# Four-layer decoder trunk on one core: the chunks of the feed-forward loop taken in pairs in layers 2 to 4

## The chip, the cores and the metric

The kernel runs on one core of one Trainium2 chip. The metric is the time of one execution on the device in microseconds. A core has TensorE (PE, with its weight loads shown apart as PEld), VectorE (DVE), ScalarE (ACT), GpSimd (POOL) and SyncE (SP), which here only issues transfers of weights. They work on their own queues, each in order, and wait for one another by semaphores.

## The reference

Four layers over x of 256 tokens by 1024 channels, in float32. Each layer has a token mixer (forgetting attention in the first and fourth, a state-space layer in the second, causal mean pooling in the third), and then a gated feed-forward part:

```python
def swiglu(x, w1, w3, w2):
    return (jax.nn.silu(x @ w1) * (x @ w3)) @ w2
...
    for i in range(DEPTH):
        ...   # m = the mixer of layer i, applied to h
        h = layer_norm(DN_ALPHA * h + m, ln_g[i, 0], ln_b[i, 0])
        h = layer_norm(DN_ALPHA * h + swiglu(h, ffn_w1[i], ffn_w3[i], ffn_w2[i]), ln_g[i, 1], ln_b[i, 1])
```

w1 and w3 are 1024 x 2816, w2 is 2816 x 1024.

## The kernel before

**Weights as tiles.** All weights are cut into 370 tiles of 128 x 1024 float32 (512 KB), numbered in the order in which they are used. Each tile goes through four steps. SyncE brings it from memory into one of four places of `raw`; it issues the transfer of tile c once the low half of tile c-4 is made. ScalarE makes the tile's high half (line 616, `whi` or `ext`, type float32r), VectorE the low half, raw minus high (line 1020). TensorE then multiplies with the halves, three products for each full one: high by high, high by low, low by high.

**Places and the ring.** A pair of halves lies in one of eight places (four in `whi`/`wlo`, four in `ext`) in this part of the program. The function `ring` deals them out in turn, and the high half of tile c waits until the tile that had the place before it has been used (`before[c]`), as a rule tile c-8. At three tiles, `SKIPS = (starts[2] - 40, starts[2] + 12, starts[3] + 12)`, the order of the places is turned by two, so the six tiles from there on take the place of the tile six back, and the two behind them that of the tile fourteen back. The first of these, starts[2]-40, is tile 26 of the second layer's feed-forward part. The other two are in the mixers of the third and fourth layer.

**The feed-forward part.** The 2816 hidden channels are 22 chunks (`FCH`) of 128. A chunk c has three tiles: up 1 (w1) makes 128 x 256 in PSUM bank 4, up 3 (w3) the same in bank 5, with 24 matmuls of 256 columns each (lines 1627 to 1629), and down (w2) adds h @ w2 into banks 0 to 3, with 14 matmuls (lines 1636 to 1661). T0 is the number of the layer's first such tile, T_FFN = 66 their count. The first two chunks are done together by other code; chunks 2 to 21 go through `up1`, `up3` and `down` on TensorE:

- up1(c) waits for silu of chunk c-1 (`silu_ready`), which has read bank 4.
- ScalarE: silu of bank 4 (line 697), after up1(c). VectorE: product of bank 5 and silu into `hval` (line 1168), after up3(c). up3(c+1) waits for it (`h_ready`).
- h is split as the weights are: ScalarE copies `hval` to h's high half (line 702), VectorE makes the low half (line 1172). down(c) waits for it (`hlo_ready`). The halves lie in `hhi`/`hlo`, two places by c % 2; the last two chunks of a layer have `h3hi`, `h3lo`, `h4hi`, `h4lo`.

The place of a tile in the order is given by `up_at(c)` (up 1; up 3 is one behind it) and `down_at(c)`. On TensorE, down(c-1) comes behind up 3 of chunk c, for c from 3 to 18. Chunks 19, 20 and 21 have their six up tiles in a row, and the remaining down tiles come last, in `tm_end`.

**What stands between on ScalarE and VectorE.** In `chunk(c)` each splits weights on the way, up to a tile given by u = T0 + up_at(c): up to u+7 ahead of silu (or of the product), up to u+8 ahead of h's half, up to u+9 behind it (the 7 is 3 + L, with L = AHEAD = 4 in layers 2 to 4). A half in that queue that has to wait for its transfer or its place holds up what is behind it:

```python
split_to(u + 3 + L)
act.wait_ge(w_used, u + 1)
nc.scalar.activation(silu[:, :], bank[4][:, 0:SEQ], ACT.Silu).then_inc(silu_ready, 1)
split_to(u + 4 + L)
```

The weights lie in memory in one order for all layers; `ffn_order` and `tile_at` say for the transfer of tile c which row of it that is.

Of the kernel before, what the change touches and what calls it, by code (L numbers as in the profile page):

```python
# [104 lines left out]
def build(nc, t, layers=DEPTH, last_ffn=True):  # L105
    starts = []
    at = 0
# [37 lines left out]
    with ExitStack() as ctx:  # L145
# [54 lines left out]
        _, far_hi, far_lo = overlay(("below_far", [P, 4 * 2 * D], F32), ("far_hi", [P, D], F32R), ("far_lo", [P, D], F32R))  # L200
        slot = [sb(f"slot{i}", [P, 2 * D]) for i in range(5)]

        def h_buf(c):
            if c == FCH - 2:
                return h3hi[:, :], h3lo[:, :]
            if c == FCH - 1:
                return h4hi[:, :], h4lo[:, :]
            return hhi[:, c % 2, :], hlo[:, c % 2, :]
        ohi, olo = overlay(("ohi", [P, KC, SEQ], F32R), ("olo", [P, KC, SEQ], F32R))
        cosT, sinT = overlay(("cosT", [P, GROUPS, NBLK], F32), ("sinT", [P, GROUPS, NBLK], F32))  # L210
        sb("held", [P, 2 * KC * SEQ])
# [32 lines left out]
            p = place[c]  # L244
            return wlo[:, p, :] if p < SPL else ext_lo[:, p - SPL, :] if p < SPL + EXT else far_lo[:, :]

        def up_at(c):

            return 2 * c if c < 3 else 3 * c - 1 if c < FCH - 2 else 2 * c + FCH - 4

        def down_at(c):

            return 6 + c if c < 2 else 3 * c + 4 if c < FCH - 4 else T_FFN - FCH + c

        def acc_banks(kind):
# [136 lines left out]
        @block.sync  # L392
        def _(sp):

            sp.dma_start(cst[:, 0:P], t["consts"][:, 0:P]).then_inc(id_landed, 16)
            sp.dma_start(x_tm[:, 0, :], t["x"][0:P, :]).then_inc(x_landed[0], 16)
            for c in range(RAW):
                sp.dma_start(raw[:, c, :], t["w"][c]).then_inc(raw_landed[c], 16)
                if c == 0:
                    sp.dma_start(x_tm[:, 1, :], t["x"][P:SEQ, :]).then_inc(x_landed[1], 16)  # L400
                if c == 1:
                    sp.dma_start(cst[:, P:], t["consts"][:, P:C_N]).then_inc(cst_landed, 16)
                    for dst, src in FIRST:
                        sp.dma_start(dst, src).then_inc(small_landed, 16)

            def toep_load(j):

                dst = toepA[:, 16 * j:16 * j + 16, :] if j < 2 else BT[:, 16 * (j - 1):16 * (j - 1) + 16, :]
                sp.dma_start(dst, t["toep"][:, j * 2 * D:(j + 1) * 2 * D].rearrange("p (g n) -> p g n", g=16)).then_inc(tp_ld[j], 16)

            def u_moves(h):

                sp.wait_ge(u1_sb, h + 1)
                for j in (2 * h, 2 * h + 1):
                    sp.dma_start(U2[32 * j + 16:32 * j + 32, :, :], u_tm[:, 1, 256 * j:256 * j + 256]).then_inc(u2_ld[h], 16)

            def toep_moves(T0):

                sp.wait_ge(m_st, 16 * 64)
                sp.wait_ge(w_used, T0 + KC)  # L420
                toep_load(0)
                toep_load(1)
                for j in (2, 3):
                    sp.wait_ge(by_n_ps, j)
                    toep_load(j)
                sp.wait_ge(by_n_ps, 4)
                for r in range(4):
                    at = r // 2 * D + r % 2 * HALF
                    sp.dma_start(bglu[32 * r:32 * r + 1, :], t["b_glu"][:, at:at + HALF]).then_inc(bglu_landed, 16)

            T1 = starts[1] if layers > 1 else n_tiles
            ffn_order = [0] * T_FFN
            for c in range(FCH):
                ffn_order[up_at(c)] = max(3 * c - 1, 0)
                ffn_order[up_at(c) + 1] = max(3 * c - 1, 0) + 1
                ffn_order[down_at(c)] = min(3 * c + 4, T_FFN - 1)

            def tile_at(c):

                for l in range(layers):  # L440
                    at = c - starts[l]
                    if MIXERS[l] == "pool" and at in range(MIX_TILES["pool"]):
                        return starts[l] + (pool_order + [KC + 1, KC + 2 + 6, KC + 2 + 7, KC] + [KC + 2 + k for k in pool_order[2:]])[at]
                    at = c - starts[l] - MIX_TILES[MIXERS[l]]
                    if at in range(T_FFN):
                        return c - at + ffn_order[at]
                return c

            for c in range(RAW, n_tiles):
                sp.wait_ge(w_lo, c - RAW + 1)  # L450
                for dst, src in LATER.get(c - KC - RAW, []):
                    sp.dma_start(dst, src).then_inc(later_landed, 16)
                if T1 <= c < T1 + KC:

                    h, k = (c - T1) // 4, T1 + 2 * ((c - T1) % 4)
                    sp.dma_start(raw[:, c % RAW, :].rearrange("p (k d) -> p k d", k=2),
                                 t["w"][k:k + 2, :, h * HALF:(h + 1) * HALF].rearrange("k p d -> p k d")).then_inc(raw_landed[c % RAW], 16)
                else:
                    sp.dma_start(raw[:, c % RAW, :], t["w"][tile_at(c)]).then_inc(raw_landed[c % RAW], 16)
                if c == T1 + 4 + RAW:  # L460
                    u_moves(0)
                if c == T1 + KC + RAW - 1:
                    u_moves(1)
                    toep_moves(T1)
            sp.wait_ge(out_ready[1], 1)
            sp.dma_start(t["out"][P:SEQ, 0:HALF], x_tm[:, 1, 0:HALF]).then_inc(stored, 16)
# [3 lines left out]
        def _(pool):  # L470
# [62 lines left out]
            def s5_turns():  # L533
# [8 lines left out]
                step(nc.gpsimd.memset(sinT[:, :, 0:1], 0.0))  # L542
                for k in (1, 2, 4, 8, 16):
                    if 2 * k == NBLK:
                        pool.wait_ge(w_used, F0 + up_at(FCH - 4))
                    n_g = min(GROUPS, HALF // k)
                    for g0 in range(0, GROUPS, n_g):
                        gs = slice(g0, g0 + n_g)
                        bc = lambda v: v[:, gs].unsqueeze(2).to_broadcast([P, n_g, k])
                        e1, e2 = (slot[0][:, i * HALF:i * HALF + n_g * k].rearrange("p (g n) -> p g n", g=n_g) for i in range(2))  # L550
                        cmul(cosT[:, gs, k:2 * k], sinT[:, gs, k:2 * k], cosT[:, gs, 0:k], sinT[:, gs, 0:k], bc(a[0]), bc(a[1]), e1, e2)
                    if 2 * k < NBLK:
                        cmul(sq[0], sq[1], a[0], a[1], a[0], a[1], r(0), r(1))
                        a, sq = sq, a
# [40 lines left out]
        def _(act):  # L595
# [76 lines left out]
            def ffn(l, n):  # L672
# [18 lines left out]

                def chunk(c):

                    u = T0 + up_at(c)
                    split_to(u + 3 + L)
                    act.wait_ge(w_used, u + 1)
                    nc.scalar.activation(silu[:, :], bank[4][:, 0:SEQ], ACT.Silu).then_inc(silu_ready, 1)  # L697
                    split_to(u + 4 + L)
                    if c == 2:
                        act.wait_ge(w_used, T0 + down_at(0) + 1)  # L700
                    act.wait_ge(h_ready, E0 + c + 1)
                    nc.scalar.activation(h_buf(c)[0], hval[:, :], ACT.Copy).then_inc(hhi_ready, 1)  # L702
                    split_to(u + 5 + L)

                def bt_block(b):
# [291 lines left out]
        def _(dve):  # L997
# [136 lines left out]
            def ffn(l, n):  # L1134
# [29 lines left out]

                def gate(c):
                    dve.wait_ge(silu_ready, E0 + c + 1)
                    dve.wait_ge(w_used, T0 + up_at(c) + 2)
                    V.tensor_tensor(hval[:, :], bank[5][:, 0:SEQ], silu[:, :], ALU.mult).then_inc(h_ready, 1)  # L1168

                def gate_lo(c):  # L1170
                    dve.wait_ge(hhi_ready, E0 + c + 1)
                    V.tensor_tensor(h_buf(c)[1], hval[:, :], h_buf(c)[0].bitcast(F32), ALU.subtract).then_inc(hlo_ready, 1)  # L1172

                def chunk(c):
                    u = T0 + up_at(c)
                    split_to(u + 3 + L)
                    if c < FCH - 1:
                        table_piece()
# [411 lines left out]
        def _(pe):  # L1590
# [132 lines left out]
            def used(ins):  # L1723
                ins.then_inc(w_used, 1)
# [79 lines left out]
            def ffn(l, n):  # L1804
# [9 lines left out]
                    ins.then_inc(hT_ps, 1)  # L1814

                def up1(c):
                    u = T0 + up_at(c)
                    pe.wait_ge(w_lo, u + 1)
                    if c > 2:
                        pe.wait_ge(silu_ready, E0 + c)  # L1820
                    used(fm(u, bank[4][:, 0:SEQ], xhi, xlo))

                def up3(c):
                    u = T0 + up_at(c) + 1
                    pe.wait_ge(w_lo, u + 1)
                    pe.wait_ge(h_ready, E0 + c)
                    used(fm(u, bank[5][:, 0:SEQ], xhi, xlo))

                def down(c):
                    t = T0 + down_at(c)  # L1830
                    pe.wait_ge(w_lo, t + 1)
                    pe.wait_ge(hlo_ready, E0 + (2 if c < 2 else c + 1))
                    used(tm_quarters(t, hhi[:, c % 2, :], hlo[:, c % 2, :], acc, c == 0))

                def bt_block(b):

# [19 lines left out]
                for c in range(3, FCH):  # L1856
                    up1(c)
                    up3(c)
                    if c < FCH - 3:
                        down(c - 1)  # L1860
                    if s5_here and 5 <= c < 13:
                        bt_block(c - 5)
# [7 lines left out]
                def ready(i):  # L1870
                    pe.wait_ge(w_lo, t + i + 1)
                    pe.wait_ge(hlo_ready, E0 + h + i + 1)
                tm_end(n + 1, [(t + i,) + h_buf(h + i) for i in range(k)], ready)

            def fox(l, f, n):
                T0 = starts[l]
# [491 lines left out]
```

## Time and profile before

| | us |
|---|---|
| median of 3 runs | 1164.77 (1163.43 to 1165.23) |
| the profiled execution | 1165.95 |
| its span, first to last instruction | 1164.2 |
| TensorE busy | 1147.3 |
| VectorE busy | 818.7 |
| ScalarE busy | 600.5 |
| mean granted TensorE clock | 0.997 |

Busy times of TensorE count the overlapping run-out of matmuls, so where it works without a pause it shows 100%, and how fast it works is read from the distance of the starts. The loops of the second, third and fourth layer lie about at 448 to 604, 689 to 845 and 992 to 1145 us of the span.

### The profile page before, as it was taken

How to read it: one execution, taken by the hardware profiler on the slowest of the kernel's cores; microseconds unless marked ns; L12 is line 12 of the kernel's file. 1: busy time of each engine (PE TensorE's matmuls, PEld its weight loads, DVE VectorE, ACT ScalarE, POOL GpSimd, SP SyncE). 2: the span in 40 equal slices, each digit the busy share in tenths (PEclk: the TensorE clock that was granted, in tenths of full speed). 3: DMA queues.
4: the chain of work that ended last, by engine and by line, in shares of the span. 5: the costliest groups of instructions: out<-in, count | busy, mean ns of one | idle time of the engine just before them, and what ended most of it. 6: DMA issues, size and time to landing. Idle time of an engine off the chain costs nothing.

```text
span 1164.2 us, 20745 instructions
## 1 busy us (share of the span) xinstructions
PE 1147.3 (99%) x8416; PEld 1033.1 (89%) x8416; DVE 818.7 (70%) x1263; ACT 600.5 (52%) x947; POOL 161.2 (14%) x212
## 2 busy tenths in 40 slices
PE   8999999999999999999999999999999999999997
PEld 7998899999877789999998889999989988999996
DVE  7789899989867687455456776554587768754545
ACT  6777444544444465454444555444438664644441
POOL 0650099102970000000000000000010000000000
PEclk9999999999999999999999999999999999999999
DMA  6676464655766558565654657656536434856550
GB/s 243 216 273 228 163 195 150 199 182 176 223 173 218 181 181 280 199 218 183 203 176 163 199 178 239 200 181 204 192 106 231 136 109 145 275 184 207 183 165 37
DMA packets 63975, 221.04 MB, mean 190 GB/s; under 512 B 8068, under 2 KB 9988, under 8 KB 63368
## 3 DMA queue, kind: packets, MB, share of 16 engines
q1 hardware_dynamic: 57224, 202.57, 53.0%
q0 software_dynamic: 5648, 15.73, 4.1%
q10 hardware_dynamic: 1008, 1.41, 0.4%
q8 instruction: 67, 1.10, 0.4%
q14 instruction: 28, 0.23, 0.1%
HBM read 211.03 MB, written 7.60 MB: 188 GB/s over the span
## 4 chain that ended last, share of the span: by engine, by line
PE 85%; DVE 9%; DMA 2%; ACT 2%; issue 1%; SPq 0%; ACTq 0%; DVEq 0%
PE bank L1627 14%; PE bank L1629 14%; PE bank L1628 14%; PE bank L1636 6%; PE bank L1638 6%; PE bank L1642 6%; PE bank L1659 5%; PE bank L1759 5%; PE bank L1693 4%; PE bank L1661 3%; DVE wlo L1020 3%; DMA raw<-in_w 2%; PE bank L1607 1%; PE bank L1794 1%; PE bank L1950 1%
## 5 line engine op out<-in xcount | busy, mean ns | idle before, releaser
L1020 DVE TENSOR_TENSOR wlo<-raw,whi 128x1024 fp32r<-128x1024 f32 x227 | 288.3, 1277 | 59.3 <-ACT whi L616 58.3
L616 ACT ACTIVATE whi<-raw 128x1024 fp32r<-128x1024 f32 x227 | 239.0, 1057 | 74.5 <-PE bank L1661 27.6
L1627 PE MATMUL bank<-xboth,whi 128*128 128x256 f32 x936 | 261.2, 279 | 0.3 <-ACT qa_late L782 0.2
L1628 PE MATMUL bank<-xboth,whi 128*128 128x256 f32 x936 | 259.0, 277 | 0.0
L1629 PE MATMUL bank<-xboth,wlo 128*128 128x256 f32 x936 | 258.8, 276 | 0.0
L1020 DVE TENSOR_TENSOR ext<-raw,ext 128x1024 fp32r<-128x1024 f32 x142 | 172.3, 1221 | 43.0 <-ACT ext L616 42.8
L1627 PEld LDWEIGHTS bank<-xboth,whi 128*128 128x128 f32 x936 | 176.0, 188 | 1.9 <-issue 1.1
L1628 PEld LDWEIGHTS bank<-xboth,whi 128*128 128x128 f32 x936 | 176.0, 188 | 0.1
L1629 PEld LDWEIGHTS bank<-xboth,wlo 128*128 128x128 f32 x936 | 175.8, 188 | 0.0
L616 ACT ACTIVATE ext<-raw 128x1024 fp32r<-128x1024 f32 x142 | 148.7, 1056 | 46.2 <-DMA raw<-in_w 22.2
L1627 PE MATMUL bank<-xboth,ext 128*128 128x256 f32 x600 | 167.4, 279 | 0.1
L1628 PE MATMUL bank<-xboth,ext 128*128 128x256 f32 x600 | 166.1, 277 | 0.0
L1629 PE MATMUL bank<-xboth,ext 128*128 128x256 f32 x600 | 166.0, 277 | 0.0
L1168 DVE TENSOR_TENSOR hval<-bank,silu 128x256 f32<-128x256 f32 x80 | 33.8, 422 | 156.3 <-PE bank L1629 156.1
L1627 PEld LDWEIGHTS bank<-xboth,ext 128*128 128x128 f32 x600 | 112.9, 188 | 1.2 <-issue 0.9
L1628 PEld LDWEIGHTS bank<-xboth,ext 128*128 128x128 f32 x600 | 112.8, 188 | 0.1
L1629 PEld LDWEIGHTS bank<-xboth,ext 128*128 128x128 f32 x600 | 112.7, 188 | 0.0
L702 ACT ACTIVATE hhi<-hval 128x256 fp32r<-128x256 f32 x72 | 30.0, 417 | 127.0 <-DVE hval L1168 124.9
L697 ACT ACTIVATE silu<-bank 128x256 f32<-128x256 f32 x80 | 30.5, 381 | 98.3 <-PE bank L1629 98.3
L583 POOL DMA_DIRECT2D slot<-in_ln_row x16 | 8.6, 543 | 447.7 <-DVE x_tm L1092 396.1
L626 ACT ACTIVATE xboth<-bank 128x256 fp32r<-128x256 f32 x64 | 21.1, 381 | 44.9 <-PE bank L1607 44.7
L1172 DVE TENSOR_TENSOR hlo<-hval,hhi 128x256 fp32r<-128x256 f32 x72 | 34.2, 474 | 0.0
(395 smaller groups left out, 2044.0 us busy)
## 6 DMA issues: line engine op xcount, KB each, us to landing
raw<-in_w SPq DMA_DIRECT2D x370, 512.0 KB, 4.2
slot<-in_ln_row POOLq DMA_DIRECT2D x16, 512.0 KB, 5.1
toep<-slot POOLq DMA_DIRECT2D x8, 512.0 KB, 8.1
toepA<-toep SPq DMA_DIRECT2D x2, 1024.0 KB, 5.8
BT<-toep SPq DMA_DIRECT2D x2, 1024.0 KB, 7.5
x_tm<-in_x SPq DMA_DIRECT2D x2, 512.0 KB, 5.1
slot<-in_s_B SPq DMA_DIRECT2D x2, 512.0 KB, 5.3
slot<-in_s_C SPq DMA_DIRECT2D x2, 512.0 KB, 5.1
```

Source lines behind the costliest of these rows:

```text
L616: nc.scalar.activation(hi_of(c), raw[:, c % RAW, :], ACT.Copy).then_inc(w_hi, 1)
L1020: V.tensor_tensor(lo_of(c), raw[:, c % RAW, :], hi_of(c).bitcast(F32), ALU.subtract).then_inc(w_lo, 1)
L1627: mm(dst, wh, bhi[:, kc, :], start=(i == 0), stop=False)
L1628: mm(dst, wh, blo[:, kc, :], start=False, stop=False)
L1629: ins = mm(dst, wl, bhi[:, kc, :], start=False, stop=(i == len(chunks) - 1))
L1636: mm(banks[2 * m + j][:, :], a_hi[:, cols], hi_of(c)[:, j * HALF:(j + 1) * HALF], start=first, stop=False)
L1638: mm(banks[2 * m + j][:, :], a_hi[:, cols], lo_of(c)[:, j * HALF:(j + 1) * HALF], start=False, stop=False)
L1642: ins = mm(banks[2 * m + j][:, :], a_lo[:, cols], hi_of(c)[:, j * HALF:(j + 1) * HALF], start=False, stop=last)
L1659: mm(banks[2 + j][:, :], a[:, cols], w[:, j * HALF:(j + 1) * HALF], start=start, stop=False)
L1661: ins = mm(banks[2 + q // 2][:, q % 2 * SEQ:(q % 2 + 1) * SEQ], a_lo[:, cols], hi_of(c)[:, q * SEQ:(q + 1) * SEQ], start=False, stop=False)
L1693: return mm(banks[b][:, :], (a_lo if lo_act else a_hi)[:, cols], (lo_of if lo_w else hi_of)(c)[:, half], start=False, stop=stop)
L1759: return mm(out, x[:, kc, m * P:(m + 1) * P], w[:, 0:4, kc * P:(kc + 1) * P], start=start, stop=stop)
```

## The change

In layers 2 to 4 (l > 0) chunks 3 to 18 are taken in pairs: up 1 and up 3 of an odd chunk, up 1 and up 3 of the even chunk behind it, and then two down tiles, those of chunks c-2 and c-1 for the even c. `up_at` and `down_at` have the layer as an argument and give the new numbers; `ffn_order` is now one list for each layer, so that the same weights arrive for each chunk. The halves of h of these layers lie in four places by c % 4: the two of `hhi`/`hlo`, and `h3hi`.. and `h4hi`... The first layer stays as it was. Ring, `SKIPS`, the number of places and the rule for the splits (u+7, u+8, u+9) stay, but since u now steps by 2 and 4 in turn instead of 3, the splits are dealt out otherwise: two ahead of an odd chunk's silu, none ahead of an even chunk's.

```diff
-        def h_buf(c):
-            if c == FCH - 2:
+        def h_buf(l, c):
+            i = c % 4 if l > 0 else c % 2 + 2 * (c >= FCH - 2)
+            if i == 2:
                 return h3hi[:, :], h3lo[:, :]
-            if c == FCH - 1:
+            if i == 3:
                 return h4hi[:, :], h4lo[:, :]
-            return hhi[:, c % 2, :], hlo[:, c % 2, :]
+            return hhi[:, i, :], hlo[:, i, :]
...
-        def up_at(c):
+        def up_at(l, c):
 
+            if l > 0 and 3 <= c < FCH - 3:
+                return 6 * ((c - 3) // 2) + 8 + 2 * ((c - 3) % 2)
             return 2 * c if c < 3 else 3 * c - 1 if c < FCH - 2 else 2 * c + FCH - 4
 
-        def down_at(c):
+        def down_at(l, c):
 
+            if l > 0 and 2 <= c < FCH - 4:
+                return 6 * ((c - 2) // 2) + 12 + (c - 2) % 2
             return 6 + c if c < 2 else 3 * c + 4 if c < FCH - 4 else T_FFN - FCH + c
...
-            ffn_order = [0] * T_FFN
-            for c in range(FCH):
-                ffn_order[up_at(c)] = max(3 * c - 1, 0)
...
+            ffn_order = [[0] * T_FFN for _ in range(layers)]
+            for l in range(layers):
+                for c in range(FCH):
+                    ffn_order[l][up_at(l, c)] = max(3 * c - 1, 0)
...
-                    used(tm_quarters(t, hhi[:, c % 2, :], hlo[:, c % 2, :], acc, c == 0))
+                    used(tm_quarters(t, *h_buf(l, c), acc, c == 0))
...
                 for c in range(3, FCH):
                     up1(c)
                     up3(c)
-                    if c < FCH - 3:
+                    if l == 0 and c < FCH - 3:
+                        down(c - 1)
+                    if l > 0 and c < FCH - 3 and c % 2 == 0:
+                        down(c - 2)
                         down(c - 1)
```

Everything else in the diff hands the layer on to these functions. The changed file is six lines longer ahead of the engines' own parts, so line 1627 of before is line 1633 of the changed kernel, 1636 is 1642, 616 is 622, 697 is 703 and 702 is 708.

TensorE at the end of up 3 of chunk 3 in the second layer (bank5 is what up 3 writes, bank4 what up 1 writes, bank0 and bank1 what a down tile writes), before:

```order
L1627 MATMUL bank5<-xboth,ext 128x256
L1628 MATMUL bank5<-xboth,ext 128x256
L1629 MATMUL bank5<-xboth,ext 128x256
L1636 MATMUL bank0<-ext,hhi 128x512 [waits hlo_ready,w_lo]
L1636 MATMUL bank1<-ext,hhi 128x512
L1638 MATMUL bank0<-ext,hhi 128x512
```

and with the change, at the same place:

```order
L1633 MATMUL bank5<-xboth,ext 128x256
L1634 MATMUL bank5<-xboth,ext 128x256
L1635 MATMUL bank5<-xboth,ext 128x256
L1633 MATMUL bank4<-xboth,ext 128x256 [waits silu_ready,w_lo]
L1634 MATMUL bank4<-xboth,ext 128x256
L1635 MATMUL bank4<-xboth,ext 128x256
```

Tile 10 of the layer was the down tile of chunk 2, which waits for h's low half; now it is up 1 of chunk 4, which waits for silu of chunk 3. The down tile stands two tiles further on, at 12.

ScalarE in the second layer from silu of chunk 6 to silu of chunk 8 (rows on `whi` and `ext` are high halves of weights; `hhi`, `h3hi` and `h4hi` are h's), before:

```order
L697 ACTIVATE silu<-bank4 128x256 [waits w_used]
L616 ACTIVATE ext<-raw 128x1024 [waits w_used,raw_landed3]
L702 ACTIVATE hhi<-hval 128x256 [waits h_ready]
L616 ACTIVATE whi<-raw 128x1024 [waits w_used,raw_landed0]
L616 ACTIVATE whi<-raw 128x1024 [waits w_used,raw_landed1]
L697 ACTIVATE silu<-bank4 128x256 [waits w_used]
L616 ACTIVATE whi<-raw 128x1024 [waits w_used,raw_landed2]
L702 ACTIVATE hhi<-hval 128x256 [waits h_ready]
L616 ACTIVATE whi<-raw 128x1024 [waits w_used,raw_landed3]
L616 ACTIVATE ext<-raw 128x1024 [waits w_used,raw_landed0]
L697 ACTIVATE silu<-bank4 128x256 [waits w_used]
```

and with the change:

```order
L703 ACTIVATE silu<-bank4 128x256 [waits w_used]
L622 ACTIVATE ext<-raw 128x1024 [waits w_used,raw_landed2]
L708 ACTIVATE h3hi<-hval 128x256 [waits h_ready]
L622 ACTIVATE ext<-raw 128x1024 [waits w_used,raw_landed3]
L622 ACTIVATE whi<-raw 128x1024 [waits w_used,raw_landed0]
L622 ACTIVATE whi<-raw 128x1024 [waits w_used,raw_landed1]
L703 ACTIVATE silu<-bank4 128x256 [waits w_used]
L622 ACTIVATE whi<-raw 128x1024 [waits w_used,raw_landed2]
L708 ACTIVATE h4hi<-hval 128x256 [waits h_ready]
L622 ACTIVATE whi<-raw 128x1024 [waits w_used,raw_landed3]
L703 ACTIVATE silu<-bank4 128x256 [waits w_used]
```

Silu of chunk 7 stands in the middle of both, and in both the two rows ahead of it are the halves of tiles 26 and 27. There are now three halves between the half of h and silu of chunk 7, and one between the half of h and silu of chunk 8.

## Rows read from the trace of the kernel before

**Rows 1.** The page's part 1: busy us, share, instructions.
```profile
PE 1147.3 (99%) x8416; PEld 1033.1 (89%) x8416; DVE 818.7 (70%) x1263; ACT 600.5 (52%) x947; POOL 161.2 (14%) x212
```

**Rows 2.** Timeline of TensorE: start, us, operation, count, [idle before]; first rows of tiles.
```profile
475.85 0.63 PE L1636 MATMUL bank<-ext,hhi 128*128 128x512 f32 x2
...
478.60 0.29 PE L1627 MATMUL bank<-xboth,ext 128*128 128x256 f32 x1
...
481.34 0.28 PE L1627 MATMUL bank<-xboth,ext 128*128 128x256 f32 x1
...
484.06 0.63 PE L1636 MATMUL bank<-ext,hhi 128*128 128x512 f32 x2
...
486.82 0.29 PE L1627 MATMUL bank<-xboth,whi 128*128 128x256 f32 x1
```

**Rows 3.** Timelines of TensorE and ScalarE, end of the second layer's loop.
```profile
590.84 0.28 PE L1627 MATMUL bank<-xboth,whi 128*128 128x256 f32 x1
...
593.56 0.28 PE L1627 MATMUL bank<-xboth,whi 128*128 128x256 f32 x1
593.75 0.39 ACT L697 ACTIVATE silu<-bank 128x256 f32<-128x256 f32 x1 [0.78 <-PE bank L1629]
...
596.28 0.28 PE L1627 MATMUL bank<-xboth,whi 128*128 128x256 f32 x1
```

**Rows 4.** Timelines of three engines, start of the second layer's loop.
```profile
448.15 0.62 PE L1636 MATMUL bank<-whi,hhi 128*128 128x512 f32 x2
450.89 0.63 PE L1636 MATMUL bank<-whi,hhi 128*128 128x512 f32 x2
453.38 0.37 ACT L697 ACTIVATE silu<-bank 128x256 f32<-128x256 f32 x1
453.89 0.36 PE L1627 MATMUL bank<-xboth,ext 128*128 128x256 f32 x1
456.70 0.28 PE L1627 MATMUL bank<-xboth,ext 128*128 128x256 f32 x1
457.40 1.07 ACT L616 ACTIVATE whi<-raw 128x1024 fp32r<-128x1024 f32 x1 [0.23 <-DMA raw<-in_w]
458.90 1.06 ACT L616 ACTIVATE whi<-raw 128x1024 fp32r<-128x1024 f32 x1 [0.43 <-DMA raw<-in_w]
459.42 0.63 PE L1636 MATMUL bank<-ext,hhi 128*128 128x512 f32 x2
459.87 0.36 ACT L697 ACTIVATE silu<-bank 128x256 f32<-128x256 f32 x1
460.00 1.23 DVE L1020 TENSOR_TENSOR wlo<-raw,whi 128x1024 fp32r<-128x1024 f32 x1 [0.20 <-ACT whi L616]
461.14 0.42 DVE L1168 TENSOR_TENSOR hval<-bank,silu 128x256 f32<-128x256 f32 x1
462.18 0.29 PE L1627 MATMUL bank<-xboth,ext 128*128 128x256 f32 x1
```

**Rows 5.** The same two moments in the third layer: end of tile 9, silu of chunk 3.
```profile
700.38 0.63 PE L1636 MATMUL bank<-ext,hhi 128*128 128x512 f32 x2
700.55 0.36 ACT L697 ACTIVATE silu<-bank 128x256 f32<-128x256 f32 x1
```

**Rows 6.** And in the fourth layer.
```profile
1003.04 0.63 PE L1636 MATMUL bank<-whi,hhi 128*128 128x512 f32 x2
1003.52 0.37 ACT L697 ACTIVATE silu<-bank 128x256 f32<-128x256 f32 x1
```

**Rows 7.** Timelines of TensorE and ScalarE, second layer, tiles 21 and 22.
```profile
489.56 0.28 PE L1627 MATMUL bank<-xboth,whi 128*128 128x256 f32 x1
492.28 0.63 PE L1636 MATMUL bank<-whi,hhi 128*128 128x512 f32 x2
492.54 1.06 ACT L616 ACTIVATE whi<-raw 128x1024 fp32r<-128x1024 f32 x1 [1.66 <-PE bank L1629]
493.50 0.36 ACT L697 ACTIVATE silu<-bank 128x256 f32<-128x256 f32 x1
495.03 0.29 PE L1627 MATMUL bank<-xboth,whi 128*128 128x256 f32 x1
```

**Rows 8.** Windows: length, busy by engine (x instructions), granted clock, DMA share, GB/s.
```profile
355.00:360.00 5.00, 4.38 (x25) 2.85 (x23) 4.85 (x7) 2.67 (x4) 0.00 (x0) 1.00 0.89 331
360.00:362.40 2.40, 1.80 (x33) 1.69 (x32) 2.27 (x4) 1.17 (x2) 0.00 (x0) 1.00 0.99 420
362.40:365.90 3.50, 3.50 (x34) 1.90 (x38) 3.34 (x7) 1.29 (x2) 0.00 (x0) 0.51 0.36 145
...
306.00:331.00 25.00, 23.28 (x242) 19.32 (x241) 19.68 (x35) 10.97 (x20) 16.64 (x32) 1.00 0.57 165
```

More of the change, by code:

```diff
@@ L431, in _ @@
             T1 = starts[1] if layers > 1 else n_tiles
-            ffn_order = [0] * T_FFN
-            for c in range(FCH):
-                ffn_order[up_at(c)] = max(3 * c - 1, 0)
-                ffn_order[up_at(c) + 1] = max(3 * c - 1, 0) + 1
-                ffn_order[down_at(c)] = min(3 * c + 4, T_FFN - 1)
+            ffn_order = [[0] * T_FFN for _ in range(layers)]
+            for l in range(layers):
+                for c in range(FCH):
+                    ffn_order[l][up_at(l, c)] = max(3 * c - 1, 0)
+                    ffn_order[l][up_at(l, c) + 1] = max(3 * c - 1, 0) + 1
+                    ffn_order[l][down_at(l, c)] = min(3 * c + 4, T_FFN - 1)
             def tile_at(c):
@@ L445, in tile_at @@
                     if at in range(T_FFN):
-                        return c - at + ffn_order[at]
+                        return c - at + ffn_order[l][at]
                 return c
@@ L544, in s5_turns @@
                     if 2 * k == NBLK:
-                        pool.wait_ge(w_used, F0 + up_at(FCH - 4))
+                        pool.wait_ge(w_used, F0 + up_at(0, FCH - 4))
                     n_g = min(GROUPS, HALF // k)
@@ L692, in chunk @@
                 def chunk(c):
-                    u = T0 + up_at(c)
+                    u = T0 + up_at(l, c)
                     split_to(u + 3 + L)
@@ L699, in chunk @@
                     if c == 2:
-                        act.wait_ge(w_used, T0 + down_at(0) + 1)
+                        act.wait_ge(w_used, T0 + down_at(l, 0) + 1)
                     act.wait_ge(h_ready, E0 + c + 1)
-                    nc.scalar.activation(h_buf(c)[0], hval[:, :], ACT.Copy).then_inc(hhi_ready, 1)
+                    nc.scalar.activation(h_buf(l, c)[0], hval[:, :], ACT.Copy).then_inc(hhi_ready, 1)
                     split_to(u + 5 + L)
@@ L1166, in gate @@
                     dve.wait_ge(silu_ready, E0 + c + 1)
-                    dve.wait_ge(w_used, T0 + up_at(c) + 2)
+                    dve.wait_ge(w_used, T0 + up_at(l, c) + 2)
                     V.tensor_tensor(hval[:, :], bank[5][:, 0:SEQ], silu[:, :], ALU.mult).then_inc(h_ready, 1)
@@ L1171, in gate_lo @@
                     dve.wait_ge(hhi_ready, E0 + c + 1)
-                    V.tensor_tensor(h_buf(c)[1], hval[:, :], h_buf(c)[0].bitcast(F32), ALU.subtract).then_inc(hlo_ready, 1)
+                    V.tensor_tensor(h_buf(l, c)[1], hval[:, :], h_buf(l, c)[0].bitcast(F32), ALU.subtract).then_inc(hlo_ready, 1)
                 def chunk(c):
-                    u = T0 + up_at(c)
+                    u = T0 + up_at(l, c)
                     split_to(u + 3 + L)
@@ L1816, in up1 @@
                 def up1(c):
-                    u = T0 + up_at(c)
+                    u = T0 + up_at(l, c)
                     pe.wait_ge(w_lo, u + 1)
@@ L1823, in up3 @@
                 def up3(c):
-                    u = T0 + up_at(c) + 1
+                    u = T0 + up_at(l, c) + 1
                     pe.wait_ge(w_lo, u + 1)
@@ L1829, in down @@
                 def down(c):
-                    t = T0 + down_at(c)
+                    t = T0 + down_at(l, c)
                     pe.wait_ge(w_lo, t + 1)
                     pe.wait_ge(hlo_ready, E0 + (2 if c < 2 else c + 1))
-                    used(tm_quarters(t, hhi[:, c % 2, :], hlo[:, c % 2, :], acc, c == 0))
+                    used(tm_quarters(t, *h_buf(l, c), acc, c == 0))
                 def bt_block(b):
@@ L1872, in ready @@
                     pe.wait_ge(hlo_ready, E0 + h + i + 1)
-                tm_end(n + 1, [(t + i,) + h_buf(h + i) for i in range(k)], ready)
+                tm_end(n + 1, [(t + i,) + h_buf(l, h + i) for i in range(k)], ready)
             def fox(l, f, n):
```

## The prediction

> **What bounds the kernel now.** I read the page first: TensorE is busy 1147.3 of 1164.2 us [rows 1], so time can only be won or lost where it stands still or works slower than it could. Then the timeline of TensorE in a quiet part of the second layer's feed-forward loop [rows 2]. One chunk is three tiles: up (into bank 4), up (into bank 5), down. The starts are 475.85 (down), 478.60 (up 1), 481.34 (up 3), 484.06 (the next down), 486.82. So a down tile takes 2.75 us, an up tile behind a down tile 2.74, an up tile behind another up tile 2.72, with no wait between them: 8.21 us a chunk. Third, what TensorE waits for if tiles are placed otherwise. An up tile into bank 4 may start once ScalarE's silu has read that bank; ScalarE does silu in the same queue as the high halves of the weights. So I read ScalarE beside TensorE at the loop's start in each of the three layers [rows 4 to 6] and at the one place in the loop where the ring of weight places turns [rows 7], and last the granted clock around TensorE's pauses [rows 8].
>
> "Stall" below is the time by which a tile starts later than the end of the one ahead; the end of a tile is taken as the start of the next in the trace. T0 is the loop's first tile in its layer, and "tile 10" means T0+10.
>
> **What goes away.** Sixteen single down tiles (those of chunks 2 to 17) become eight pairs, in three layers: 24 times an up tile comes behind an up tile instead of a down tile, and 24 times a down tile behind a down tile. The first is worth 2.74-2.72 = 0.02 us each [rows 2], 24 x 0.02 = 0.48 us. The second I cost at nothing: the one pair of down tiles of the loop today, at its start, has 450.89-448.15 = 2.74 us for the first [rows 4], beside 2.75 in the quiet part; a hundredth per pair would be 0.2 us, inside the range.
>
> The Trainium skill ("TensorE: Matmul & The Clock Gate", Step-by-step: what each phase is for) says TensorE pulls weight loads ahead of running matmuls, by which a switch of tile kind would cost nothing. The rows show a remainder of 0.02 us at a switch; by the rule the gain would be 0, and the sum 0.48 us higher.
>
> **What a tile of slack was worth.** Before, up 1 of chunk c+1 came behind a down tile, so silu of chunk c had an up tile and a down tile (5.47 us) to finish. Now, for odd c from 3 to 17, up 1 of the even chunk comes straight behind up 3 of c, and silu has one up tile, 2.72 us. Where silu is prompt that is enough: the end of the layer runs so already. Up tiles start at 590.84, 593.56 and 596.28, silu of the first is at 593.75, done at 594.14, and bank 4 is written again at 596.28, 2.1 us later; both steps are 2.72 us [rows 3]. In the new order the two high halves ahead of an odd chunk's silu need the two down tiles ahead of it, the later one used by the time up 1 starts; that half runs 1.06 us in a tile of 2.74. So in most of the loop there is no stall. It is different in two kinds of place.
>
> (1) The loop's start. In the second layer up 3 of chunk 3 ends at 459.42. Silu of chunk 3 starts at 459.87 and takes 0.36, since ScalarE first makes the halves of tiles 14 (457.40) and 15 (458.90), both held back by the landing of the weights ("<-DMA raw") [rows 4]. Today a down tile covers this: up 1 of chunk 4 starts at 462.18. In the new order it would want to start at 459.42. How long from silu's end to the matmul? The same wait is in the trace one chunk earlier: silu of chunk 2 ends at 453.38+0.37 = 453.75, up 1 of chunk 3 starts at 453.89, so 0.14. The new start is 459.87+0.36+0.14 = 460.37, a stall of 0.95. The part ahead of it (weights, queues of ScalarE and VectorE) is the same up to there, so these times hold. Third layer: 700.55+0.36+0.14 = 701.05 against 700.38, 0.67 [rows 5]. Fourth: 1003.52+0.37+0.14 = 1004.03 against 1003.04, 0.99 [rows 6]. Sum 2.61 us. What is behind it is late by the same and nothing more: the gate product of chunk 3 ends at 461.14+0.42 = 461.56 [rows 4], and up 3 of chunk 4 wants it at 460.37+2.8 = 463.2; the down tiles of 2 and 3 follow at 465.9, and then the queues have their lead back.
>
> (2) The turn of the ring, second layer, tile 26. Normally a half waits for the tile eight back. `SKIPS` turns the order of places by two at T0+26, so tiles 26 to 31 wait for the one six back: the half of 27 waits for tile 21, which is up 3 of chunk 7 itself. ScalarE has that half in its queue ahead of silu of chunk 7, before and after. In the trace tile 21 runs from 489.56 to 492.28, the half of 27 starts at 492.54, silu at 493.50, done at 493.86 [rows 7]. Today the down tile hides it (up 1 of chunk 8 at 495.03). In the new order tile 22 is up 1 of chunk 8: it starts at 493.50+0.36+0.14 = 494.00 instead of 492.28, a stall of 1.72. The next such places are harmless: the half of 29 waits for up 3 of chunk 8 ahead of silu 8, but two down tiles (5.5 us) follow; 30 and 31 wait for these. The other two turns lie outside the loops.
>
> A tile that starts after a stall is slower: 453.89 to 456.70 is 2.81 against 2.72 [rows 2, 4]. Four times 0.09 is 0.36.
>
> VectorE follows the same pattern with two halves ahead of an odd gate product; in 5.5 us it has two low halves, a gate product and h's low half, 3.3 us by its rows (1.23 each for low halves, 0.42 for the others [rows 4]). h's four places take no wait away that TensorE saw: at 459.42 the down tile was ready to go.
>
> **Sum.** 2.61 + 1.72 + 0.36 - 0.48 = +4.2 us. On the profiled execution's 1165.95 us (span 1164.2) that is 1170.2; that execution lay 1.18 above the median of the runs, and on the median, 1164.77, it is 1169.0. Bounds: the three starts hang on when two transfers land. If they landed 1 us earlier all of 2.61 would go; 0.4 us later each would add 1.2. The ring's stall hangs on TensorE alone and is firm.
>
> **Rivals.** (A) the sum above.
>
> (B) Only the ring's stall: the starts vary with the landings, and silu of chunk 3 is in time in all three layers. 1.72+0.09-0.48 = +1.3, 1166.1. For it: the waits on landings are short, 0.23 and 0.43 us [rows 4]. Against: the same lateness in three layers, 0.67 to 0.99.
>
> (C) Not slower: silu of chunk 7 is not held by tile 21. If the half of tile 27 could be made before 492.28-1.5, nothing stalls there, and if the starts are prompt too only the 0.48 us are left: 1164.3. It decides at 490.8 on this trace. For it: the weights of tile 27 need not be late, since no transfer is named in that wait. Against: the half of 27 started 0.26 us after up 3's end, with ScalarE idle 1.66 us ahead of it and TensorE named as its releaser [rows 7].
>
> (D) A bubble at every pair. One bank for each of the two up products is emptied in 2.72 us instead of 5.47; if ScalarE got to silu late everywhere as at the starts (0.67 to 0.99, mean 0.87, with 0.09 behind it), 24 pairs cost 24 x 0.96 = 23.0; with 0.9 more for the ring's and less 0.5 that is 1188. Against: [rows 3], no bubble in the same order. The Trainium skill ("Perfetto Trace Analysis", Optimizing Tensor Performance) wants independent matmul groups to rotate through banks so that the emptying of one overlaps the next, and under Optimization Strategy it takes a repeated bubble as a sign of too few buffers; that rule speaks against this change, since the freed slack is just that overlap. By the rule the time is this rival's; the rows at the layer's end say that two banks are enough when silu is prompt.
>
> (E) The clock. TensorE stands still 1.72 us at one place. Once in this trace the granted clock went to 0.51 for 3.5 us (level 1.2 of 2.4 GHz), after 355 to 362.4 us, in which TensorE was busy 4.38 of 5 and 1.80 of 2.40 us with small matmuls. From 306 to 331 it also paused, 23.28 of 25 busy, and the clock stayed at 1.00 [rows 8]. A drop would cost half of 3.5, 1.7 us more: 1170.7. Against: dense tiles on both sides of the stall.
>
> **Numbers.** A 0.81, B 0.08, C 0.03, D 0.03, E 0.05. No more than 0.2% (2.3 us) from before is "the same", which is about what a measurement of this kernel can tell; B and a tail of A fall in it. Slower 0.88, same 0.09, faster 0.03. Range: A with half its start stalls is 1167.7, B is 1166.1; upward A with later landings 1170.3, E 1170.7. I take 1166.7 to 1170.9, which leaves out C, D and B.
>
> **What would show it.** In the changed kernel's trace: up 1 of chunk 4 in each of the three layers starts 0.7 to 1.0 us after up 3 of chunk 3 has ended, 0.14 after silu; up 1 of chunk 8 in the second layer about 1.7 us after; no gap at other pairs; up tiles of 2.72 three times in four. Chunks 9 to 18 of a layer then take 16.40 us a pair (2.74 + 3 x 2.72 + 2 x 2.75) instead of 16.42. Wrong would be: no gap at chunk 8 of the second layer, a gap at pairs in the middle of the third and fourth layers, or a low clock near 494.

## The result, and the profile after

| | before | changed |
|---|---|---|
| median, us | 1164.77 (5 runs, 1163.43 to 1166.21) | 1169.7 (5 runs, 1168.06 to 1172.64) |
| profiled execution, its span | 1165.95, 1164.2 | 1169.01, 1167.2 |

The ratio of changed to before is 1.0047, 95% interval 1.0035 to 1.0058: the kernel is slower by 5.5 us (4.1 to 6.8). The forecast was +4.2.

The page after, its first part and the largest group of matmuls of its fifth part (busy, mean ns, then the idle time ahead of them and what ended it):

```profile
PE 1147.7 (98%) x8416; PEld 1033.5 (89%) x8416; DVE 818.8 (70%) x1263; ACT 600.8 (51%) x947; POOL 161.0 (14%) x212
...
L1633 PE MATMUL bank<-xboth,whi 128*128 128x256 f32 x944 | 263.2, 279 | 1.9 <-ACT silu L703 1.9
```

Beside [rows 1] the instructions are as many and the busy times differ by 0.4 us at most, while the span is 3.0 us longer: TensorE has no more to do, it stands still. The group's idle time names the one who lets it go on, silu. Groups show little more: 1.9 us is one of two such groups (that of `ext` has 2.0), and shows neither place nor cause. For that come the timelines. A pair in the quiet part of the second layer, the same view as [rows 2]:

```profile
470.22 0.29 PE L1633 MATMUL bank<-xboth,whi 128*128 128x256 f32 x1
...
472.96 0.28 PE L1633 MATMUL bank<-xboth,whi 128*128 128x256 f32 x1
...
475.68 0.28 PE L1633 MATMUL bank<-xboth,ext 128*128 128x256 f32 x1
...
478.40 0.28 PE L1633 MATMUL bank<-xboth,ext 128*128 128x256 f32 x1
...
481.12 0.63 PE L1642 MATMUL bank<-ext,hhi 128*128 128x512 f32 x2
...
483.87 0.63 PE L1642 MATMUL bank<-ext,hhi 128*128 128x512 f32 x2
...
486.64 0.29 PE L1633 MATMUL bank<-xboth,whi 128*128 128x256 f32 x1
```

Up tiles of 2.74, 2.72, 2.72 and 2.72, down tiles of 2.75 and 2.77: 16.42 us a pair, no stall. Two chunks of before took 16.43 (470.39 to 486.82), and 16.40 was forecast. The start of the loop in the second layer, TensorE and ScalarE, answers to [rows 4]:

```profile
455.28 0.28 PE L1633 MATMUL bank<-xboth,ext 128*128 128x256 f32 x1
...
455.88 1.07 ACT L622 ACTIVATE whi<-raw 128x1024 fp32r<-128x1024 f32 x1 [0.24 <-DMA raw<-in_w]
...
457.51 1.06 ACT L622 ACTIVATE whi<-raw 128x1024 fp32r<-128x1024 f32 x1 [0.56 <-DMA raw<-in_w]
458.48 0.36 ACT L703 ACTIVATE silu<-bank 128x256 f32<-128x256 f32 x1
458.99 0.36 PE L1633 MATMUL bank<-xboth,ext 128*128 128x256 f32 x1 [0.82 <-ACT silu L703]
...
461.89 0.28 PE L1633 MATMUL bank<-xboth,ext 128*128 128x256 f32 x1
```

Up 3 of chunk 3 starts at 455.28 and takes 2.72, to 458.00. Silu ends at 458.84, the next up 1 starts 0.15 later, at 458.99: a stall of 0.99 (0.95 forecast). The trace writes [0.82], since it counts idle time from the modelled end of the last matmul and not from where the next could have started; stalls here are from start to start. The third and the fourth layer, against [rows 5, 6]:

```profile
699.77 0.28 PE L1633 MATMUL bank<-xboth,ext 128*128 128x256 f32 x1
...
703.07 0.37 ACT L703 ACTIVATE silu<-bank 128x256 f32<-128x256 f32 x1
...
703.58 0.36 PE L1633 MATMUL bank<-xboth,ext 128*128 128x256 f32 x1 [0.93 <-ACT silu L703]
...
1002.63 0.28 PE L1633 MATMUL bank<-xboth,whi 128*128 128x256 f32 x1
...
1005.34 0.36 ACT L703 ACTIVATE silu<-bank 128x256 f32<-128x256 f32 x1
1005.84 0.36 PE L1633 MATMUL bank<-xboth,whi 128*128 128x256 f32 x1 [0.34 <-ACT silu L703]
```

3.81-2.72 = 1.09, and 0.50 (3.218 unrounded, less 2.72). And the turn of the ring, against [rows 7]:

```profile
489.38 0.28 PE L1633 MATMUL bank<-xboth,whi 128*128 128x256 f32 x1
...
492.36 1.06 ACT L622 ACTIVATE whi<-raw 128x1024 fp32r<-128x1024 f32 x1 [1.66 <-PE bank L1635]
493.32 0.36 ACT L703 ACTIVATE silu<-bank 128x256 f32<-128x256 f32 x1
493.83 0.36 PE L1633 MATMUL bank<-xboth,whi 128*128 128x256 f32 x1 [1.57 <-ACT silu L703]
...
496.65 0.28 PE L1633 MATMUL bank<-xboth,whi 128*128 128x256 f32 x1
```

The half of tile 27 starts 0.26 after up 3 of chunk 7 has ended (492.10), silu 0.96 behind it, up 1 of chunk 8 0.51 behind that: 493.83-489.38-2.72 = 1.73 us. The window around it (columns as in [rows 8]) shows that the granted clock did not fall:

```profile
492.00:494.00 2.00, 0.43 (x4) 0.26 (x3) 0.58 (x2) 1.33 (x2) 0.00 (x0) 1.00 0.48 182
498.00:502.00 4.00, 4.00 (x27) 3.60 (x26) 2.83 (x4) 1.61 (x3) 0.00 (x0) 1.00 0.40 134
```

To compare kernels I use the length of each loop, from the start of up 3 of chunk 2 to the first matmul of the end part. It leaves out what the mixers and layer norms do differently from one execution to the next.

| loop, us | layer 2 | layer 3 | layer 4 | sum |
|---|---|---|---|---|
| before | 159.23 | 158.86 | 156.39 | 474.48 |
| changed | 162.19 | 160.43 | 156.91 | 479.53 |

The three loops are 5.05 us longer, the span only 3.0: between the first and the second layer's loop the profiled execution of the changed kernel gained 1.7 us on that of before (marks 0.4 us later at 312, 1.3 us earlier at 417), and 0.8 in the fourth layer's mixer, parts that the change does not touch. Of the 1.7, 1.6 us come between 350 and 366 us, and the windows tell why: the granted clock of before was 0.51 in the 3.5 us from 362.40 [rows 8], and here it is 1.00 in the same stretch (columns as in [rows 8]):

```profile
362.40:365.90 3.50, 3.12 (x68) 2.17 (x69) 3.28 (x8) 2.60 (x4) 0.00 (x0) 1.00 0.15 59
```

Of the eleven kernels' profiled executions in this document, five have such a drop of 3.4 us, starting between 361 and 364 us (before, e1, e2, e7, e8), the others none. A lower clock weighs in the timed executions, too, though they do not show where it fell: in one batch of 29 executions of the kernel before, the 18 with a mean granted clock of 0.998 or 0.999 have a mean of 1163.97 us, the 11 with 0.996 or 0.997 one of 1166.17. What the 0.8 us are is open. The interval of the timed ratio holds 5.05 and not 3.0.

### The profile page after: what moved, and what is told of

Same layout as the page of the kernel before. It is cut to its first block, busy times and chain, and to the rows that moved or that the text cites. A ratio compares the mean times of both kernels' runs of the same rounds, so it can differ in the third digit from the quotient of the medians.

```text
span 1167.2 us, 20721 instructions
## 1 busy us (share of the span) xinstructions
PE 1147.7 (98%) x8416; PEld 1033.5 (89%) x8416; DVE 818.8 (70%) x1263; ACT 600.8 (51%) x947; POOL 161.0 (14%) x212
## 4 chain that ended last, share of the span: by engine, by line
PE 81%; DVE 10%; DMA 4%; ACT 2%; issue 2%; SPq 0%; ACTq 0%; DVEq 0%
PE bank L1633 13%; PE bank L1634 13%; PE bank L1635 13%; PE bank L1642 6%; PE bank L1644 5%; PE bank L1648 5%; PE bank L1665 5%; PE bank L1765 5%; DMA raw<-in_w 4%; PE bank L1699 4%; DVE wlo L1026 3%; PE bank L1667 3%; PE bank L1613 1%; PE bank L1800 1%; DVE ext L1026 1%
## 5 line engine op out<-in xcount | busy, mean ns | idle before, releaser
L1633 PE MATMUL bank<-xboth,ext 128*128 128x256 f32 x592 | 165.3, 279 | 2.0 <-ACT silu L703 2.0
L1634 PE MATMUL bank<-xboth,ext 128*128 128x256 f32 x592 | 163.9, 277 | 0.0
L1635 PE MATMUL bank<-xboth,ext 128*128 128x256 f32 x592 | 163.9, 277 | 0.0
L1633 PEld LDWEIGHTS bank<-xboth,ext 128*128 128x128 f32 x592 | 111.3, 188 | 3.6 <-issue 2.6
L1634 PEld LDWEIGHTS bank<-xboth,ext 128*128 128x128 f32 x592 | 111.3, 188 | 0.1
L1635 PEld LDWEIGHTS bank<-xboth,ext 128*128 128x128 f32 x592 | 111.3, 188 | 0.0
L708 ACT ACTIVATE hhi<-hval 128x256 fp32r<-128x256 f32 x48 | 20.1, 419 | 97.6 <-DVE hval L1174 95.5
L1765 PE MATMUL bank<-whi,xboth 128*128 128x512 f32 x96 | 32.0, 404 | 0.0
```

Of the source, the lines that this page charges most:

```text
L1633: mm(dst, wh, bhi[:, kc, :], start=(i == 0), stop=False)
L1634: mm(dst, wh, blo[:, kc, :], start=False, stop=False)
L1635: ins = mm(dst, wl, bhi[:, kc, :], start=False, stop=(i == len(chunks) - 1))
L1765: return mm(out, x[:, kc, m * P:(m + 1) * P], w[:, 0:4, kc * P:(kc + 1) * P], start=start, stop=stop)
```

## The experiments

Theory S, the prediction's: an up 1 stalls where silu of the odd chunk stands in ScalarE's queue behind a weight half that is late, because its transfer lands late (starts) or because it waits for a tile just in use (the ring's turn). All edits are to the changed kernel unless said otherwise.

### e1_turn: the ring turned elsewhere

```diff
-    SKIPS = (starts[2] - 40, starts[2] + 12, starts[3] + 12)
+    SKIPS = (starts[1] + T_S5 + 4, starts[2] + 12, starts[3] + 12)
```

> The changed kernel with one number moved: the first turn of the ring stands at the second layer's T0+4 instead of T0+26, where the six tiles with the shorter distance wait for tiles that the loop's opening has used anyway. Theory S (up 1 of an even chunk stalls only where silu of the odd chunk is queued behind a late weight half; the ring's turn makes one such half late): the stall of 1.73 us before up 1 of chunk 8 in the second layer is gone, the three stalls at chunk 4 stay (sum 2.2 to 2.9), and the kernel is 1.8 us faster than the changed one: before + 3.1, about 1167.9. Rival M (the ring is not the cause, bank 4 is emptied too late there): the stall stays and the time is that of the changed kernel, before + 4.9.

Measured: ratio 1.0033 (1.0021 to 1.0046), +3.8 us (2.4 to 5.4), median 1168.07. In the trace ScalarE makes silu of chunk 7 with nothing in its way:

```profile
488.65 1.06 ACT L622 ACTIVATE whi<-raw 128x1024 fp32r<-128x1024 f32 x1 [1.70 <-PE bank L1667]
491.33 0.38 ACT L703 ACTIVATE silu<-bank 128x256 f32<-128x256 f32 x1 [1.62 <-PE bank L1635]
491.61 1.05 ACT L622 ACTIVATE whi<-raw 128x1024 fp32r<-128x1024 f32 x1
```

It is now let go by up 1 (491.13) and not by up 3; up tiles start at 488.39, 491.13, 493.85 and 496.57, no stall. The three stalls at chunk 4 stay, with 1.03, 1.25 and 1.35 us: 3.6 in sum, more than the 2.9 allowed for. It is the trace that puts M out; the time alone does not, as its interval holds both S's +3.1 and M's +4.9, and the loops of this execution are only 0.4 us shorter in sum (479.09) than the changed kernel's.

### e2_start: pairs from chunk 5 on

```diff
-            if l > 0 and 3 <= c < FCH - 3:
+            if l > 0 and 5 <= c < FCH - 3:
...
-            if l > 0 and 2 <= c < FCH - 4:
+            if l > 0 and 4 <= c < FCH - 4:
...
-                    if l == 0 and c < FCH - 3:
+                    if c < (FCH - 3 if l == 0 else 5):
                         down(c - 1)
-                    if l > 0 and c < FCH - 3 and c % 2 == 0:
+                    if l > 0 and 5 < c < FCH - 3 and c % 2 == 0:
```

> The changed kernel with the pairs beginning at chunk 5 instead of 3: chunks 3 and 4 have one down tile behind each, as before the change, in layers 2 to 4; the ring is as in the changed kernel. Theory S: the three stalls at chunk 4 (0.99, 1.09, 0.50 us) and the slower up tiles behind them (0.6) are gone, the ring's stays: before + 1.8, about 1166.6; no new stall at chunk 6, since silu of chunk 5 is not late in the kernel before in any layer. Rival P (the first pair is late wherever it stands, because the pairing itself starves ScalarE): stalls of 0.5 to 1 us appear before up 1 of chunk 6 instead, and the time stays at before + 4 to + 5.

Measured: ratio 1.0024 (1.0011 to 1.0038), +2.8 us (1.3 to 4.4), median 1168.28. No stall at chunk 4 nor at chunk 6 in any layer, and the ring's stall is there, 1.73 us (490.25 to 494.71 for a tile of 2.72). P is out by the trace; the time, with an interval up to +4.4, would just allow its +4. The profiled execution had two waits that belong to neither, before up 1 of chunk 3: 0.65 us in the second layer and 2.3 in the third. They come on top of the ring's stall in this execution; the timed +2.8 still has the expected +1.8 in its interval. The rows of the third layer show silu of chunk 2, which stood behind the half of tile 11 and that behind its landing:

```profile
698.43 1.06 ACT L622 ACTIVATE ext<-raw 128x1024 fp32r<-128x1024 f32 x1 [3.75 <-DMA raw<-in_w]
699.39 0.37 ACT L703 ACTIVATE silu<-bank 128x256 f32<-128x256 f32 x1
```

The kernel before has this wait at chunk 3 too, 0.24 and 0.22 us in the second and fourth layer. It became the matter of the last experiments.

### e3_both

Both edits together.

> Both edits: ring turned at T0+4, and pairs from chunk 5 on. Theory S: no stall of an up 1 in the paired part at all; what is left is the switch of tile kinds, 21 pairs of -0.019 +0.012 us by the trace of the changed kernel, that is -0.15: before - 0.15 with a quarter of a per cent of scatter, ratio within 0.998 to 1.002. Rival M (something else in the pairing costs too, as the slower up tiles of 2.80 to 2.90 us): before + 1 to + 2.

Measured: ratio 0.9993 (0.9983 to 1.0003), median 1164.52. No stall in the paired part. The loops are 159.79, 159.36 and 156.60, of which 0.67, 0.22 and 0.23 us are the wait at chunk 3. So the two causes are all of the loss that timing can measure.

### e4_queue: silu one place earlier in the queue

```diff
-                    split_to(u + 3 + L)
+                    split_to(u + 3 + L - (1 if l > 0 and c % 2 and 3 <= c < FCH - 3 else 0))
```

in `chunk` of ScalarE and of VectorE; order of tiles, pairs and ring are those of the changed kernel.

> The changed kernel, all pairs and the ring's turn as in it; only the queues differ: ScalarE and VectorE make one weight half less ahead of silu and of the gate product of an odd chunk 3 to 17 in layers 2 to 4, and that half behind it. Theory S: the ring's stall is gone, since the half that waits for up 3 of chunk 7 is now behind silu 7; at the starts silu of chunk 3 is behind the half of tile 14 alone and starts 1.4 us earlier, so these stalls are gone or below 0.1: before + 0 to + 0.4. Rival B (one bank is too little: 2.7 us do not suffice to empty it): the stalls stay, before + 4 to + 5. Rival G (the late half then holds the gate product or h's half instead): stalls move to up 3 of the even chunk, before + 1 to + 3.

Measured: ratio 0.9997 (0.9988 to 1.0006), median 1164.58. All four stalls are gone. ScalarE at the turn of the ring:

```profile
486.98 1.06 ACT L622 ACTIVATE whi<-raw 128x1024 fp32r<-128x1024 f32 x1 [6.39 <-PE bank L1635]
487.94 0.36 ACT L703 ACTIVATE silu<-bank 128x256 f32<-128x256 f32 x1
489.70 1.06 ACT L622 ACTIVATE whi<-raw 128x1024 fp32r<-128x1024 f32 x1 [1.39 <-PE bank L1635]
```

The half of tile 27 still waits for up 3 of chunk 7 and starts 0.26 after it has ended (489.44), but silu has been done since 488.30, and up 1 of chunk 8 starts at 489.44. Bank 4 is emptied in one up tile's time in all 24 pairs, so rival B here, and (D) of the prediction, are out; and so is G, as no up 3 of an even chunk is late.

### e6_turn28: the turn two tiles later (one execution)

```diff
-    SKIPS = (starts[2] - 40, starts[2] + 12, starts[3] + 12)
+    SKIPS = (starts[2] - 38, starts[2] + 12, starts[3] + 12)
```

> The changed kernel with the ring's first turn two tiles later, at T0+28 of the second layer. The six tiles with the shorter distance are then 28 to 33, and the one whose half stands ahead of an odd chunk's silu and waits for that chunk's own up 3 is 33, ahead of silu of chunk 9. Theory S: no stall before up 1 of chunk 8; one of 1.73 us before up 1 of chunk 10. Rival M (chunk 8 is late for a reason of its own place in the layer): the stall stays at chunk 8.

Measured: 1169.02 us. The stall has moved with the turn. Chunk 8 runs without one (491.74 to 494.46), and up 1 of chunk 10 is late:

```profile
505.44 0.28 PE L1633 MATMUL bank<-xboth,ext 128*128 128x256 f32 x1
...
509.89 0.36 PE L1633 MATMUL bank<-xboth,whi 128*128 128x256 f32 x1 [1.57 <-ACT silu L703]
```

509.89-505.44-2.72 = 1.73 us, and ScalarE makes the half of tile 33 at 508.42 and silu at 509.38, in the order foretold. This is the sharpest of the tests, as it says where a stall must appear and how long it must be. It rests on the trace; one execution's time says nothing.

### e5_before_turn and e7_places: each part alone in the kernel before

e5 has e1's edit in the kernel before. e7 has the new `h_buf(l, c)` and its uses there, with the old order of tiles.

> The kernel before, with only the ring's first turn moved from T0+26 to T0+4 of the second layer. Theory S: in the order of before a down tile covers the late silu of chunk 7, so the turn cost nothing there and moving it gains nothing: ratio 1.000, and silu of chunk 7 then starts about 0.3 us behind the end of up 1 of chunk 7 instead of 3.9 us behind it. Rival R (the turn costs time by itself, in both kernels): 1.5 us faster than before, ratio 0.9987.

> The kernel before, with only h's halves in four places by chunk number in layers 2 to 4, order of tiles unchanged. Theory S: no wait of TensorE hangs on h's places in either order, ratio 1.000 within 0.15%. Rival H (the places in another region of memory change how fast a down tile reads its stationary halves, or take a wait away): down tiles of chunks on h3hi and h4hi differ from 2.75 us by more than 0.02, and the time moves by 24 such tiles a layer or more than 1 us.

Measured: e5 0.9995 (0.9983 to 1.0006), e7 0.9994 (0.9981 to 1.0007): no difference for either. In e5 silu of chunk 7 starts 0.20 after the end of up 1 of that chunk at 486.75; before it was 3.94 behind.

```profile
486.95 0.38 ACT L697 ACTIVATE silu<-bank 128x256 f32<-128x256 f32 x1 [1.62 <-PE bank L1629]
```

The kernel before thus carried the late silu at no cost, and the down tile was its cover. In e7 no down tile is off 2.75 by more than 0.02, but for those that TensorE's wait at chunk 3 follows. Neither R nor H.

### e8_queue_c2 and e9_before_c2: the wait at chunk 3, too

e8 is e4 with chunk 2 among the chunks whose silu goes one half earlier. e9 is the kernel before with chunk 2 alone:

```diff
-                    split_to(u + 3 + L)
+                    split_to(u + 3 + L - (1 if l > 0 and c == 2 else 0))
```

> The version with one weight half less ahead of silu and the gate product of odd chunks, and the same for chunk 2, in layers 2 to 4. Silu of chunk 2 then no longer stands behind the half of tile 11, whose landing set it 0.24 to 0.65 us late in the second layer in the traces so far (and up to 2.33 in the third). Theory S: no stall of an up 1 anywhere in the loops of layers 2 to 4, against before 0.3 to 1 us less there: ratio 0.998 to 1.000. Rival L (the late landing shows up one step later, at the low half of a weight tile or at silu of chunk 3): stalls of the same size at chunks 3 or 4, ratio as without it, 0.9997.

> The kernel before, order of tiles unchanged, with one weight half less ahead of silu and of the gate product of chunk 2 alone, in layers 2 to 4. It tells where the 0.15% of the version with prompt silu in chunk 2 and pairs come from. Theory S: from chunk 2's wait, the pairs give 0.1 to 0.2 us at most, so this kernel has loops of 158.9 to 159.1, 158.8 to 159.0 and 156.1 to 156.2 us (second up tile of chunk 2's predecessor to the end part), no stall before up 1 of chunk 3, and ratio 0.9985 to 0.9998. Rival Q (the pairs give the gain once silu is prompt): the loops stay at 159.2 and 156.4 and the ratio is 1.000.

Measured: e8 0.9985 (0.9973 to 0.9998), median 1163.52 against 1164.71; e9 0.9979 (0.9967 to 0.9990), median 1162.79 against 1165.75. Both beat the kernel before and the changed one. In e8's second layer:

```profile
448.79 1.06 ACT L622 ACTIVATE ext<-raw 128x1024 fp32r<-128x1024 f32 x1 [0.68 <-DMA raw<-in_w]
449.76 0.36 ACT L703 ACTIVATE silu<-bank 128x256 f32<-128x256 f32 x1
451.55 1.06 ACT L622 ACTIVATE ext<-raw 128x1024 fp32r<-128x1024 f32 x1 [1.43 <-DMA raw<-in_w]
```

The half of tile 11 waits for its landing until 451.55 and no longer holds silu, done at 450.12; up 1 of chunk 3 starts at 453.02 without a stall. No up tile stalls anywhere in the three loops.

| loop, us | layer 2 | layer 3 | layer 4 | sum |
|---|---|---|---|---|
| e4_queue | 159.20 | 159.33 | 156.05 | 474.58 |
| e8_queue_c2 | 158.87 | 158.81 | 156.05 | 473.73 |
| e9_before_c2 | 158.92 | 158.92 | 156.17 | 474.01 |

e8 and e9 differ by the 24 pairs and by 0.28 us in the sum of the loops, of which the opening tile has 0.15. By the traces what the loops gain is chunk 2's, and the pairs give 0.1 to 0.2 us, which timing can't tell (the intervals of e4, e8 and e9 overlap). Of the 0.85 us by which e8's loops are shorter than e4's, only 0.3 were a stall; 0.5 were slow up tiles in the third layer, which are shown in the last section. Theory S holds for the traces, Q and L don't.

The time of e9 is another matter. Its ratio of 0.9979 lies below the 0.9985 to 0.9998 that was expected. The edit is the only difference, so the gain of 1.2 to 3.8 us is its own, but the loops explain 0.5 us of it (0.7 and 0.9 against the traces of e5 and e7, whose order of tiles is also that of before). The rest is open: landings late by more, as the 2.3 us in e2, would weigh in some executions, but that was not counted over runs.

## Why the prediction was right, point by point

**The sum.** All terms, forecast against what the two traces show:

| term | forecast | measured |
|---|---|---|
| start stalls, layers 2, 3, 4 | 0.95, 0.67, 0.99 | 0.99, 1.09, 0.50 |
| the ring's stall | 1.72 | 1.73 |
| slower tiles behind stalls | 0.36 | 0.77 |
| switches of tile kind | -0.48 | -0.17 |
| the wait at chunk 3, already there | 0 | +0.14 |
| sum | +4.2 | +5.05 |

The measured column is of the loops in the two profiled executions; the timed difference is +5.5 (4.1 to 6.8).

**Start stalls.** The three sum to 2.58 (2.61 forecast), but one by one the third layer's is 0.42 too long and the fourth's 0.49 too short, as they hang on landings. That the sum agrees is luck: it is 3.6 in e1 and 3.0 in e6, where the same starts stand in the same order. The prediction's "these times hold" did not hold. Place, cause and the 0.14 from silu's end to the matmul were right, and e2 and e4 take them away in two ways, by another order on TensorE and by another order on ScalarE.

**The ring.** Right to 0.01 us. It hangs on no landing: 0.26, 0.96, 0.36 and 0.15 us are steps between TensorE and ScalarE alone, and it was 1.73 in all three traces that have it (the changed kernel, e2, e6). e1, e4 and e6 show the cause.

**Slower tiles behind a stall** is the term that was sized too small. I took one up tile of 2.81 for each stall. After two of four it was 2.90, and the tile behind it 2.83: 0.10 for the stalls in the ring and in the third layer's start, 0.29 for the other two.

**Switches.** The first half was right, 0.02 per up tile. The second I had put at nothing from one pair at the loop's start; the second down tile of a pair takes 2.766 against 2.754, so 24 x (0.019-0.012) = 0.17 is left. The Trainium skill ("TensorE: Matmul & The Clock Gate", Step-by-step: what each phase is for) says that weight loads are pulled ahead of running matmuls; read as "a switch costs nothing", it gives 0, which is nearer to 0.17 than my 0.48, though the trace does have 0.019 and 0.012 at the switches.

**Rivals.** B (the starts in time) and C (silu of chunk 7 free) did not come; D fell by the quiet pairs and by e4; the clock (E) stayed at 1.00 over the stall. On D the rule of the Trainium skill ("Perfetto Trace Analysis", Optimizing Tensor Performance), that the emptying of one bank should overlap the next group's matmuls, was no wrong warning: with one tile instead of two for that overlap, a late silu showed on TensorE at four places, as stalls of 0.5 to 1.7 us. But two banks do, as e4 shows, when no late half stands ahead of silu.

## What to carry to other kernels

When the order on a saturated engine is changed, first list what the work now moved away was covering: for each wait, when its releaser is done in the present trace, and how long before it is needed. A queue that mixes short steps that others wait for with long steps that may wait themselves (transfers, ring places) should have the short ones first, as early as their input allows; that made the new order harmless here (e4), and gave the old one 0.2% (0.1 to 0.33) in time (e9), of which its loops explain 0.5 to 0.9 us. A special case in a table of places, such as a turn of a ring, needs to be looked at tile by tile, for its cost depends on which step it meets.

## What the runs showed of the hardware

Behind a start that waited for silu the matmuls of 256 columns do not always resume with their distance of 0.113 us. There are two forms. In one the first up tile takes 2.80 to 2.82 us instead of 2.72 and the next 2.72. In the other the distance is 0.118 until the next down tile: the first up tile takes 2.90 and those behind it 2.83. A stall is not needed for that. In the third layer of e4, where the down tile ahead of chunk 3 took its usual 2.76, all four up tiles of chunks 3 and 4 are slow, 0.50 us in sum:

```profile
692.22 0.35 PE L1633 MATMUL bank<-xboth,ext 128*128 128x256 f32 x1
...
695.11 0.28 PE L1633 MATMUL bank<-xboth,ext 128*128 128x256 f32 x1
...
697.94 0.28 PE L1633 MATMUL bank<-xboth,ext 128*128 128x256 f32 x1
...
700.77 0.28 PE L1633 MATMUL bank<-xboth,ext 128*128 128x256 f32 x1
...
703.59 0.39 PE L1642 MATMUL bank<-whi,h3hi 128*128 128x512 f32 x1
```

The granted clock was 1.00 there. Both forms also follow stalls of the same length (1.73 us in the changed kernel and in e2), so the length does not decide; what does is open. In e8 and e9, where silu of chunk 2 is prompt, no up tile of the three loops is slow.

The landing of the weights at the loops' starts differs between executions by more than I had expected: in the nine traces without the edit of e8 and e9, up 1 of chunk 3 stalled by 0 to 0.67 us in 26 of 27 starts, and once by 2.3.
